# Expert down projection in a hybrid-decoder step: gated values stationary, weights streamed in fp32r halves, two scatters

## The chip, the cores and the metric

The kernel runs on one core of one Trainium2 chip. The metric is the device time of one execution in microseconds, the median over several runs. A difference under 0.3% is not told from none here.

## The reference, cut to what matters

A one-layer decoder step over 1088 tokens (1024 of a prompt, 64 samples): mixers, an output projection, then a mixture of experts, then a norm. The change touches the mixture alone. Each token goes to 2 of 16 experts; an expert is a gated MLP of width 512 on rows of 1024.

```python
def body(acc, params):
    wg, wu, wd, c = params
    y = (jax.nn.silu(x @ wg) * (x @ wu)) @ wd
    return acc + c[:, None] * y.astype(jnp.float32), None

acc, _ = lax.scan(body, jnp.zeros((N, D), jnp.float32), (w_gate, w_up, w_down, combine.T))
```

All inputs and weights are float32. Each expert has 2 MB each of gate, up and down weights.

## The kernel before

**Stages.** `b1_all` and `b2_all` do the mixers, output projection, second norm and router, and write the normed rows to the DRAM tensor `h2_rows` and the residual to `sums`. `b3_all` (L1408) runs the experts, `b4_all` norms the result and writes it out.

**The expert loop.** Every engine runs the same loop, one step for each expert and round. A step handles at most W = 160 of the expert's tokens: 128 as full rows, and W2 = 32 more. It takes 16 steps here (one round of 16 experts). The router has left `rank_m` (each token's place within its expert) and `table` (token numbers and routing weights, in bf16 parts).

- **Indices.** VectorE makes a one-hot matrix `oh` (`onehot`, L1621, a TENSOR_TENSOR compare of `iota_w` with `rank_m`, 2304 elements a partition); TensorE multiplies it with `facts` (`indices`, L1511); VectorE turns the sums into gather indices `idx`, scatter rows `dest` and weights `weight` (`indices`, L1630 to L1646). This runs a step or two ahead, so `dest_now` and `weight_now` (L1686, L1687) keep the copy of the step under way.
- **Gather.** POOL issues three indirect DMAs from `h2_rows` for the next step (L1468): 128 full rows, and twice 128 quarters for the other 32 rows (each row is cut in eight parts of 128, spread over the partitions). Ahead of each gather and scatter it runs a small TENSOR_TENSOR, `hold` (L1481).
- **Rows in.** TensorE transposes the gathered rows (`rows_in`, L1515) and VectorE copies them to `xT` (`x_out`, L1663).
- **Gate and up.** `gate_up(f)` for f = 0 to 3 (L1525): 16 fp32 matmuls of 128 x 128 weights (stationary, from `ring`) with `xT` (160 columns moving). ScalarE takes the Silu into `sg` (L1600), VectorE multiplies into `hid` (L1680). The banks 0 and 1 alternate, so `gate_up(f)` waits until hid(f-2) has been read out. In what follows hid(f) is the VectorE instruction for that f.
- **Down.** `down(j)`, j = 0 to 3 (L1535): eight matmuls each, down weights stationary, `hid` moving (160 columns); the result is transposed (model dimension on the partitions). ScalarE and VectorE copy it to `yT` and `yT2` (L1604, L1695).
- **Rows back.** `rows_back(h)` (L1546) transposes `yT` back to token rows, ScalarE scales with the routing weight into `yr` and `yr2` (L1615).
- **Scatter.** POOL issues three indirect DMAs that add to `sums` (L1475): 512 KB, and two of 64 KB in 512-byte parts. Then it waits until all have landed (`e_out`, L1503) and only then raises `e_free`. VectorE waits for `e_free` at f = 0 before it overwrites `dest_now`, and ScalarE before it overwrites `yr`.
- **Weights.** SP loads the next expert's weights in six transfers of 1 MB (L1453 to L1459): units 0 to 3 into `ring` (0 and 1 after gate_up(1), 2 and 3 after gate_up(3)), 4 and 5 (the two halves of `w_down`, by columns) into `wdn`, 4 after down(1), 5 after down(3). They are issued in the order 0 to 5, each behind its wait.

**Order within a step on TensorE.** gate_up 0 to 3, down 0, down 1, `rows_in` for the next step, down 2, `rows_back(0)`, down 3, `indices`, `rows_back(1)`. On VectorE: `onehot`, hid(0), then the wait for `e_free`, `dest_now`, `indices`, `lower`, then hid(1) to hid(3), yT copies and `x_out`. Each engine works its own list in order, and all waits are on semaphores written out by hand.

On fp32r: a float32 operand cast to that type is rounded; the output projection in `b2_all` (L1194 to L1196) splits each operand into a rounded half (`hi`, by a ScalarE cast) and the remainder (`lo`, by a VectorE subtraction) and adds three products.

Of the kernel before, what the change touches and what calls it, by code (L numbers as in the profile page):

```python
# [22 lines left out]
P = 128  # L23
D = 1024
# [1374 lines left out]
def expert_unit(A, ring, wdn, u, e):  # L1399

    if u < 4:
        w = (A["w_gate"], A["w_up"])[u % 2].rearrange("l e (k p) n -> (l e) p k n", p=P)
        return ring[:, u, :, :], w[e, :, :, (u // 2) * 256:(u // 2 + 1) * 256]
    w = A["w_down"].rearrange("l e (k p) n -> (l e) p k n", p=P)
    return wdn[:, u - 4, :].rearrange("p (k n) -> p k n", k=4), w[e, :, :, (u - 4) * 512:(u - 3) * 512]


def b3_all(nc, A, sb, sem, e_w, ring, wdn, bank, ident, h2_dram, sums_dram, rank_m, table, iota_w, steps):  # L1408
# [13 lines left out]
    dest = sb("dest", [P, 3], I32, ctx=c3)  # L1422
    dest_now = sb("dest_now", [P, 3], I32, ctx=c3)
# [4 lines left out]
    hid = sb("hid", [P, 4, W], ctx=c3)  # L1428
    yT = sb("yT", [P, KC, P], ctx=c3)
    yT2 = sb("yT2", [P, KC, W2], ctx=c3)  # L1430
    yr = sb("yr", [P, D], ctx=c3)
    yr2 = sb("yr2", [P, 2, P], ctx=c3)
# [9 lines left out]
    e_yt, e_ya, e_yd = sem("e_yt"), sem("e_ya"), sem("e_yd")  # L1442
    e_yr, e_re, e_out = sem("e_yr"), sem("e_re"), sem("e_out")
# [18 lines left out]
    def _(pool):  # L1462
        h2_parts = h2_dram.rearrange("t (c d) -> (t c) d", d=P)
        sums_parts = sums_dram.rearrange("t (c d) -> (t c) d", d=P)
# [27 lines left out]
        with pool.Fori(0, n) as i:  # L1492
# [14 lines left out]
    def _(pe):  # L1507
# [7 lines left out]
        def rows_in():  # L1515
            for h in range(2):
                for k in range(4):
                    x = nc.tensor.transpose(bank[4 + h][:, k * P:(k + 1) * P],
# [16 lines left out]
        def down(j, i):  # L1535
            for q in range(2):
                d = 2 * j + q
                for k in range(4):
                    if j == 0 and q == 0 and k >= 2:
                        pe.wait_ge(e_h, i * 4 + k + 2)  # L1540
                    x = nc.tensor.matmul(bank[2 + j % 2][:, q * 256:q * 256 + W],  # L1541
                                         wdn[:, d // 4, k * 512 + (d % 4) * P:k * 512 + (d % 4 + 1) * P],
                                         hid[:, k, :], start=k == 0, stop=k == 3)
            x.then_inc(e_yt, 1)

        def rows_back(h):  # L1546

            for k in range(4):
                x = nc.tensor.transpose(bank[4 + h][:, k * P:(k + 1) * P], yT[:, 4 * h + k, :], ident[:])  # L1549
            x.then_inc(e_yr, 1)  # L1550
            nc.tensor.transpose(bank[6][:, h * P:(h + 1) * P], yT2[:, 4 * h:4 * h + 4, :], ident[:]).then_inc(e_yr, 1)
# [9 lines left out]
        with pe.Fori(0, n) as i:  # L1561
            pe.wait_ge(e_xe, i * 3 + 3)
            for f in range(4):
                pe.wait_ge(e_h, i * 4 + (1 if f < 2 else f))
# [4 lines left out]
            for j in range(4):  # L1569

                pe.wait_ge(e_ya if j % 2 == 0 else e_yd, i * 2 + j // 2 + 1)
                if j % 2 == 0:
                    pe.wait_ge(e_w[4 + j // 2], i * 16 + 16)
                down(j, i)
                if j == 1:
                    pe.wait_ge(e_xg, i * 48 + 96)
                    pe.wait_ge(e_re, i * 4 + 1)
                    rows_in()
                elif j == 2:
                    pe.wait_ge(e_xe, i * 3 + 6)  # L1580
                    pe.wait_ge(e_ya, i * 2 + 2)
                    pe.wait_ge(e_yd, i * 2 + 2)
                    rows_back(0)
# [3 lines left out]
            pe.wait_ge(e_ya, i * 2 + 3)  # L1587
            pe.wait_ge(e_yd, i * 2 + 3)
            pe.wait_ge(e_re, i * 4 + 3)
            rows_back(1)  # L1590

    @blk.scalar
    def _(act):
        n = count(act)
        act.sem_inc(e_ya, 1)
        act.sem_inc(e_re, 1)
        with act.Fori(0, n) as i:
            for f in range(4):
                act.wait_ge(e_gu, i * 4 + f + 1)
                nc.scalar.activation(sg[:, f % 2, :], bank[f % 2][:, 0:W], ACT.Silu).then_inc(e_si, 1)  # L1600
            for j in (0, 2):
                act.wait_ge(e_yt, i * 4 + j + 1)
                y = bank[2][:, :].rearrange("p (q t) -> p q t", q=2)
                nc.scalar.copy(yT[:, 2 * j:2 * j + 2, :], y[:, :, 0:P])  # L1604
                nc.scalar.copy(yT2[:, 2 * j:2 * j + 2, :], y[:, :, P:W]).then_inc(e_ya, 1)
            act.wait_ge(e_free, i + 1)
            act.wait_ge(e_now, i * 2 + 2)
            for h in range(2):
                for c in range(2):
                    act.wait_ge(e_yr, i * 4 + 2 * h + c + 1)  # L1610
                    if c == 0:
                        dst, src = yr[:, h * 512:(h + 1) * 512], bank[4 + h][:, :]
                    else:
                        dst, src = yr2[:, h, :], bank[6][:, h * P:(h + 1) * P]
                    nc.scalar.activation(dst, src, ACT.Copy, scale=weight_now[:, c:c + 1]).then_inc(e_re, 1)  # L1615

    @blk.vector
    def _(dve):
# [11 lines left out]
        def indices(s):  # L1630
# [12 lines left out]
            for where, out in ((to, dest), (tok, idx)):  # L1643
                nc.vector.tensor_copy(out[:, 0:1], where[:, 0:1])
                x = nc.vector.scalar_tensor_tensor(out=out[:, 1:3], in0=where[:, 1:2].broadcast_to([P, 2]),
                                                   scalar=float(KC), in1=chunk[:], op0=ALU.mult, op1=ALU.add)  # L1646
            x.then_inc(e_idx, 1)

        n = count(dve)
        dve.sem_inc(e_h, 1)  # L1650
        dve.sem_inc(e_yd, 1)
# [22 lines left out]
        with dve.Fori(0, n) as i:  # L1674
# [109 lines left out]
```

## Time and profile before

| | |
|---|---|
| runs of the kernel | 1059.4, 1059.9, 1062.76 us; median 1059.9 |
| profiled execution, span from first to last instruction | 1055.8 us |
| TensorE matmul busy | 948.9 us, 90% |
| VectorE busy | 398.3 us, 38% |
| ScalarE busy | 294.9 us, 28% |
| POOL busy | 153.7 us, 15% |
| HBM read, written | 141.18 MB, 25.31 MB |
| mean granted TensorE clock over the span | 0.944 |

The profile is of one execution; its span is 4.1 us under the median of the runs. Busy time is the union of an engine's instructions; matmuls are pipelined, so the distance between the starts of two tells more than their length. The views used here are the page (40 slices), the timeline (instructions in order, with runs of like ones merged), groups by line, waits, and windows (busy time, clock and DMA share of a stretch).

### The profile page before, as it was taken

To read this page: it belongs to the slowest core of one execution; us is meant where nothing else is said; L and a number is where in the kernel's file an instruction comes from. 1 tells how busy PE (TensorE), PEld (TensorE's weight loads), DVE (VectorE), ACT (ScalarE), POOL (GpSimd) and SP (SyncE) were. 2 spreads that over 40 slices of the span, in tenths; PEclk is the share of its full clock that TensorE was granted. 3 is DMA by queue.
4 is the path that set the end of the run, shared out by engine and by line. 5 is a ranking of instruction groups with operands and counts; after the bars stand their busy time and mean duration, and the time that the engine had idled before them with its cause. 6 is when DMAs were issued, how large, how long until landed. Compare 5 with 4: busy or idle time off the path is not lost. (4 is left out here: it accounts for less than half of the span.)

```text
span 1055.8 us, 15299 instructions
## 1 busy us (share of the span) xinstructions
PE 948.9 (90%) x5909; PEld 814.1 (77%) x5909; DVE 398.3 (38%) x977; ACT 294.9 (28%) x573; POOL 153.7 (15%) x173
## 2 busy tenths in 40 slices
PE   5997999999999979999279999999999999999940
PEld 3567776667676658787179999999999999999930
DVE  4236733435664553543632222122222222122204
ACT  4346312443353331543101111112111121112115
POOL 1000000000000010000022322333332322233310
PEclk9998998999999979999579999999999999999975
DMA  8210105101010172543028888888878888887619
GB/s 281 94 41 1 40 1 119 34 7 41 1 40 1 46 240 77 196 163 120 21 85 235 275 266 256 264 240 243 255 237 241 271 267 261 263 245 241 173 23 355
DMA packets 124147, 165.25 MB, mean 157 GB/s; under 512 B 11872, under 2 KB 95872, under 8 KB 124117
## 3 DMA queue, kind: packets, MB, share of 16 engines
q1 hardware_dynamic: 113669, 144.76, 41.4%
q0 software_dynamic: 10448, 20.08, 8.8%
q8 instruction: 20, 0.33, 0.1%
q14 instruction: 10, 0.08, 0.0%
HBM read 141.18 MB, written 25.31 MB: 158 GB/s over the span
## 5 line engine op out<-in xcount | busy, mean ns | idle before, releaser
L1530 PE MATMUL bank<-xT,ring 128*128 128x160 f32 x2048 | 283.9, 301 | 1.8 <-DVE xT L1670 1.0
L1530 PEld LDWEIGHTS bank<-xT,ring 128*128 128x128 f32 x2048 | 280.5, 191 | 5.3 <-issue 5.3
L411 PE MATMUL bank<-hT,ring 128*128 128x384 f32 (+1 forms) x480 | 159.9, 490 | 0.0
L1541 PE MATMUL bank<-hid,wdn 128*128 128x160 f32 x1024 | 150.2, 301 | 0.0
L1541 PEld LDWEIGHTS bank<-hid,wdn 128*128 128x128 f32 x1024 | 141.3, 190 | 2.8 <-DVE hid L1680 2.8
L411 PEld LDWEIGHTS bank<-hT,ring 128*128 128x128 f32 x480 | 94.4, 200 | 57.4 <-issue 11.0
L1600 ACT ACTIVATE sg<-bank 128x160 f32<-128x160 f32 x64 | 19.5, 304 | 252.5 <-PE bank L1530 252.5
L1680 DVE TENSOR_TENSOR hid<-sg,bank 128x160 f32<-128x160 f32 x64 | 20.4, 319 | 163.0 <-ACT sg L1600 163.0
L1475 POOL DMA_INDIRECT sums<-yr,dest_now x48 | 76.2, 1587 | 12.6 <-issue 12.6
L1481 POOL TENSOR_TENSOR hold_at<-ident 128x1 f32<-128x1 f32 x32 | 18.7, 585 | 314.2 <-ACT yr L1615 250.4
L1194 PE MATMUL bank<-whi,ahi 128*128 128x512 f32 (+1 forms) x144 | 58.0, 403 | 6.2 <-DVE wlo L1293 6.1
L1695 DVE COPY yT<-bank 128x256 f32<-128x256 f32 x32 | 13.6, 424 | 124.8 <-PE bank L1541 124.8
L1196 PE MATMUL bank<-whi,alo 128*128 128x512 f32 (+1 forms) x144 | 57.1, 397 | 0.0
L1195 PE MATMUL bank<-wlo,ahi 128*128 128x512 f32 (+1 forms) x144 | 57.1, 397 | 0.0
L1468 POOL DMA_INDIRECT xg<-h_rows,idx x51 | 52.2, 1023 | 24.2 <-issue 20.2
L1621 DVE TENSOR_TENSOR oh<-iota_w,rank_m 128x2304 bf16<-128x2304 f32 x18 | 46.0, 2558 | 0.0
L1604 ACT COPY yT<-bank 128x256 f32<-128x256 f32 x32 | 11.9, 373 | 112.4 <-PE bank L1541 112.4
L1615 ACT ACTIVATE yr<-bank,weight_now 128x512 f32<-128x512 f32 x64 | 30.3, 524 | 41.8 <-PE bank L1549 41.6
L1194 PEld LDWEIGHTS bank<-whi,ahi 128*128 128x128 f32 (+1 forms) x144 | 26.9, 187 | 13.6 <-DVE alo L1287 6.7
L1196 PEld LDWEIGHTS bank<-whi,alo 128*128 128x128 f32 (+1 forms) x144 | 26.7, 186 | 6.9
L1195 PEld LDWEIGHTS bank<-wlo,ahi 128*128 128x128 f32 (+1 forms) x144 | 26.9, 187 | 6.5
L1104 POOL MEMSET before<- 128x128 bf16 x1 | 0.2, 205 | 214.3 <-POOLq L1041 214.3
(284 smaller groups left out, 1201.2 us busy)
## 6 DMA issues: line engine op xcount, KB each, us to landing
wdn<-in_w_down SPq DMA_DIRECT2D x32, 1024.0 KB, 6.9
ring<-in_w_gate SPq DMA_DIRECT2D x32, 1024.0 KB, 5.3
ring<-in_w_up SPq DMA_DIRECT2D x32, 1024.0 KB, 8.0
x<-in_x_prompt SPq DMA_DIRECT2D x16, 512.0 KB, 7.1
ring<-in_w_in SPq DMA_DIRECT2D x8, 1024.0 KB, 8.6
ring<-in_w_out SPq DMA_DIRECT2D x4, 1024.0 KB, 5.0
h_rows<-h SPq DMA_DIRECT2D x8, 512.0 KB, 2.7
sums<-x SPq DMA_DIRECT2D x8, 512.0 KB, 3.6
```

What stands on the lines that cost most here:

```text
L411: mm = nc.tensor.matmul(acc(n)[:, 0:tn], ring[:, u % 4, k, c0:c0 + P], hT[:, k, t0:t0 + tn], start=k == 0, stop=k == KC - 1)
L1194: nc.tensor.matmul(out, ahi[:, s, k, 0:r], whi[:, k, :], start=k == 0, stop=False)
L1195: nc.tensor.matmul(out, ahi[:, s, k, 0:r], wlo[:, k, :], start=False, stop=False)
L1196: m = nc.tensor.matmul(out, alo[:, s, k, 0:r], whi[:, k, :], start=False, stop=k == KC - 1)
L1468: nc.gpsimd.indirect_dma_start(out=dst, out_offset=None, in_=src, in_offset=bass.IndirectOffsetOnAxis(ap=idx[:, j:j + 1], axis=0)).then_in ...
L1475: nc.gpsimd.indirect_dma_start(out=dst, in_=src, in_offset=None, bounds_check=rows - 1, out_offset=bass.IndirectOffsetOnAxis(ap=dest_now[: ...
L1530: x = nc.tensor.matmul(bank[f % 2][:, side * 256:side * 256 + W], ring[:, u, k, c0:c0 + P], xT[:, k, :], start=k == 0, stop=k == KC - 1)
L1541: x = nc.tensor.matmul(bank[2 + j % 2][:, q * 256:q * 256 + W], wdn[:, d // 4, k * 512 + (d % 4) * P:k * 512 + (d % 4 + 1) * P], hid[:, k, ...
L1600: nc.scalar.activation(sg[:, f % 2, :], bank[f % 2][:, 0:W], ACT.Silu).then_inc(e_si, 1)
L1615: nc.scalar.activation(dst, src, ACT.Copy, scale=weight_now[:, c:c + 1]).then_inc(e_re, 1)
L1621: nc.vector.tensor_tensor(oh[:], iota_w[:].unsqueeze(1).broadcast_to([P, TT, 2 * P]), rank_m[:, bass.ds(e * TT, TT)].unsqueeze(2).broadcas ...
L1680: nc.vector.tensor_tensor(hid[:, f, :], sg[:, f % 2, :], bank[f % 2][:, 256:256 + W], ALU.mult).then_inc(e_h, 1)
```

## The change

- The down projection is turned round. `hid` becomes the stationary operand and the down weights stream, 512 columns at a time, so the result has token rows on the partitions, and `rows_back`, `yT` and `yT2` go.
- Both operands are split in fp32r halves. Weights: `wdhi` by a ScalarE copy of 128 x 1024, `wdlo` by a VectorE subtraction, four of each a step; here called cast(f) and wdlo(f). Gated values: `hs` holds hi of 128 tokens, hi of the 32 others, lo of the 32, lo of the 128; a ScalarE copy and two small VectorE subtractions for each f, called hs(f) and lo(f). For each k and each half of the columns there are five matmuls: hi·whi, hi·wlo, lo·whi for 128 tokens, and for the other 32 a stationary operand of 64 columns (their hi and lo beside one another) with whi and wlo.
- Eviction: ScalarE scales rows 32 to 63 of the second bank into `yll` and the 128 rows into `yr`; VectorE scales rows 0 to 31, adds `yll`, and writes `yl`. Two of each a step.
- Two scatters (512 KB and 128 KB) take the place of three; `dest` has two columns, and two index operations go.
- `w_down` is loaded by rows (4 KB runs) instead of by columns (2 KB). SP's order becomes 4, 0, 1, 5, 2, 3; unit 4 waits for wdlo(1), unit 5 for wdlo(3).
- `rows_in` uses the banks 0 and 1 and waits for hid(3).

```diff
-    return wdn[:, u - 4, :].rearrange("p (k n) -> p k n", k=4), w[e, :, :, (u - 4) * 512:(u - 3) * 512]
+    return wdn[:, u - 4, :].rearrange("p (k n) -> p k n", k=2), w[e, :, 2 * (u - 4):2 * (u - 3), :]
...
-            for u in range(6):
-                sp.wait_ge(e_gu if u < 4 else e_yt, i * 4 + (2 if u in (0, 1, 4) else 4))
+            for u in (4, 0, 1, 5, 2, 3):
+                sp.wait_ge(e_gu if u < 4 else e_wl, i * 4 + (2 if u in (0, 1, 4) else 4))
...
+            for j, (src, r) in enumerate(((yr[:], P), (yl[:], W2))):
+                nc.gpsimd.indirect_dma_start(out=sums_dram, in_=src, in_offset=None, bounds_check=N - 1,
+                                             out_offset=bass.IndirectOffsetOnAxis(ap=dest_now[0:r, j:j + 1], axis=0),
...
-            pool.wait_ge(e_re, i * 4 + 5)
+            pool.wait_ge(e_ye, i * 2 + 3)
+            pool.wait_ge(e_yl, i * 2 + 3)
...
-            pool.wait_ge(e_out, i * 48 + 48)
+            pool.wait_ge(e_out, i * 32 + 32)
...
+        def down(k):
+            hi, lo, last = hs[:, k, 0:P], hs[:, k, W + W2:2 * W], hs[:, k, P:W + W2]
+            for h in range(2):
+                whi, wlo = [w[:, k, h * 512:(h + 1) * 512] for w in (wdhi, wdlo)]
+                nc.tensor.matmul(bank[2 + h][:, :], hi, whi, start=k == 0, stop=False)
+                nc.tensor.matmul(bank[2 + h][:, :], hi, wlo, start=False, stop=False)
+                nc.tensor.matmul(bank[2 + h][:, :], lo, whi, start=False, stop=k == 3)
+                nc.tensor.matmul(bank[4 + h][0:2 * W2, :], last, whi, start=k == 0, stop=False)
+                x = nc.tensor.matmul(bank[4 + h][0:2 * W2, :], last, wlo, start=False, stop=k == 3)
+                if k == 3:
+                    x.then_inc(e_y, 1)
...
-                pe.wait_ge(e_h, i * 4 + (1 if f < 2 else f))
+                if f >= 2:
+                    pe.wait_ge(e_h, i * 4 + f - 1)
...
+            for k in range(4):
+                pe.wait_ge(e_wl, i * 4 + k + 1)
+                pe.wait_ge(e_hl, i * 4 + k + 1)
+                if k == 0:
+                    pe.wait_ge(e_ye, i * 2 + 1)
+                    pe.wait_ge(e_yl, i * 2 + 1)
+                down(k)
+                if k == 1:
+                    pe.wait_ge(e_xg, i * 48 + 96)
+                    pe.wait_ge(e_h, i * 4 + 4)
+                    rows_in()
...
             for f in range(4):
+                if f % 2 == 0:
+                    act.wait_ge(e_w[4 + f // 2], i * 16 + 16)
+                nc.scalar.copy(wdhi[:, f, :], wdn[:, f // 2, (f % 2) * D:(f % 2 + 1) * D]).then_inc(e_wh, 1)
                 act.wait_ge(e_gu, i * 4 + f + 1)
                 nc.scalar.activation(sg[:, f % 2, :], bank[f % 2][:, 0:W], ACT.Silu).then_inc(e_si, 1)
+                act.wait_ge(e_h, i * 4 + f + 1)
+                nc.scalar.copy(hs[:, f, 0:W], hid[:, f % 2, :]).then_inc(e_hh, 1)
...
+                act.wait_ge(e_y, i * 2 + h + 1)
+                nc.scalar.activation(yll[:, h * 512:(h + 1) * 512], bank[4 + h][W2:2 * W2, :], ACT.Copy,
+                                     scale=weight_now[W2:2 * W2, 1:2]).then_inc(e_yll, 1)
+                nc.scalar.activation(yr[:, h * 512:(h + 1) * 512], bank[2 + h][:, :], ACT.Copy,
+                                     scale=weight_now[:, 0:1]).then_inc(e_ye, 1)
...
             for f in range(4):
+                dve.wait_ge(e_wh, i * 4 + f + 1)
+                nc.vector.tensor_tensor(wdlo[:, f, :], wdn[:, f // 2, (f % 2) * D:(f % 2 + 1) * D],
+                                        wdhi[:, f, :].bitcast(F32), ALU.subtract).then_inc(e_wl, 1)
                 dve.wait_ge(e_si, i * 4 + f + 1)
-                nc.vector.tensor_tensor(hid[:, f, :], sg[:, f % 2, :], bank[f % 2][:, 256:256 + W],
+                nc.vector.tensor_tensor(hid[:, f % 2, :], sg[:, f % 2, :], bank[f % 2][:, 256:256 + W],
                                         ALU.mult).then_inc(e_h, 1)
+                dve.wait_ge(e_hh, i * 4 + f + 1)
+                nc.vector.tensor_tensor(hs[:, f, W:W + W2], hid[:, f % 2, P:W], hs[:, f, P:W].bitcast(F32), ALU.subtract)
+                nc.vector.tensor_tensor(hs[:, f, W + W2:2 * W], hid[:, f % 2, 0:P], hs[:, f, 0:P].bitcast(F32),
+                                        ALU.subtract).then_inc(e_hl, 1)
...
+            x_out(i * 3 + 3)
+            for h in range(2):
+                dve.wait_ge(e_yll, i * 2 + h + 1)
+                nc.vector.scalar_tensor_tensor(out=yl[:, h * 512:(h + 1) * 512], in0=bank[4 + h][0:W2, :],
+                                               scalar=weight_now[0:W2, 1:2], in1=yll[:, h * 512:(h + 1) * 512],
+                                               op0=ALU.mult, op1=ALU.add).then_inc(e_yl, 1)
```

## Rows read from the trace of the kernel before

**Rows 1.** The page, part 2: 40 equal slices of the span, busy tenths and granted clock.

```profile
PE   5997999999999979999279999999999999999940
...
PEclk9998998999999979999579999999999999999975
```

**Rows 2.** Timeline of TensorE, one step: start us, us, engine, line, operation.

```profile
717.70 17.62 PE L1530 MATMUL bank<-xT,ring 128*128 128x160 f32 x128
735.16 4.71 PE L1541 MATMUL bank<-hid,wdn 128*128 128x160 f32 x32
739.70 1.04 PE L1518 MATMUL bank<-ident,xg 128*128 128x128 f32 x8
...
740.80 2.34 PE L1541 MATMUL bank<-hid,wdn 128*128 128x160 f32 x16
742.97 0.60 PE L1549 MATMUL bank<-ident,yT 128*128 128x128 f32 x4
...
743.52 2.34 PE L1541 MATMUL bank<-hid,wdn 128*128 128x160 f32 x16
745.69 0.60 PE L1511 MATMUL bank<-facts,oh 128*128 128x5 bf16 x18
746.55 0.63 PE L1549 MATMUL bank<-ident,yT 128*128 128x128 f32 x4 [0.26 <-issue]
...
747.33 12.87 PE L1530 MATMUL bank<-xT,ring 128*128 128x160 f32 x93
```

**Rows 3.** Waits, 560 to 1000 us: us in total, times, longest us.

```profile
DVE dest_now L1686 <- POOLq L1503: 58.6, 15, 4.3
```

**Rows 4.** Timeline of all engines from 734 to 766 us.

```profile
746.66 2.56 DVE L1621 TENSOR_TENSOR oh<-iota_w,rank_m 128x2304 bf16<-128x2304 f32 x1
...
748.24 1.03 POOL L1481 TENSOR_TENSOR hold_at<-ident 128x1 f32<-128x1 f32 x1 [15.23 <-ACT yr L1615]
...
749.42 1.62 POOL L1475 DMA_INDIRECT sums<-yr,dest_now  x1 [0.15 <-issue]
...
756.48 0.37 SPq L1459 DMA_DIRECT2D ring<-in_w_gate  x1
...
756.58 0.17 DVE L1686 COPY dest_now<-dest 128x3 int32<-128x3 int32 x1 [3.96 <-POOLq L1503]
...
758.00 0.31 DVE L1680 TENSOR_TENSOR hid<-sg,bank 128x160 f32<-128x160 f32 x1
```

**Rows 5.** Timeline of TensorE in the output projection, fp32r, 512 columns.

```profile
454.04 0.39 PE L1194 MATMUL bank<-whi,ahi 128*128 128x512 f32 x1
...
454.72 0.39 PE L1194 MATMUL bank<-whi,ahi 128*128 128x512 f32 x1
...
459.34 0.49 PE L1194 MATMUL bank<-whi,ahi 128*128 128x512 f32 x1
```

**Rows 6.** Groups by line and shape: busy us, mean ns, idle before.

```profile
L1615 ACT ACTIVATE yr<-bank,weight_now 128x512 f32<-128x512 f32 x32 | 22.0, 688 | 41.8 <-PE bank L1549 41.6
...
L1253 ACT ACTIVATE h<-x 128x1024 f32<-128x1024 f32 x8 | 8.5, 1058 | 33.2 <-DVE x L1303 33.2
...
L1001 DVE TENSOR_TENSOR gT<-gT,v 128x1024 f32<-128x1024 f32 x4 | 4.7, 1218 | 2.5 <-ACT gT L710 2.5
```

**Rows 7.** Timeline at the start of the expert stage, VectorE and POOL.

```profile
526.74 2.55 DVE L1621 TENSOR_TENSOR oh<-iota_w,rank_m 128x2304 bf16<-128x2304 f32 x1
...
527.04 3.28 POOL L1468 DMA_INDIRECT xg<-h_rows,idx  x1 [3.94 <-DVE idx L1645]
...
530.63 0.96 POOL L1468 DMA_INDIRECT xg<-h_rows,idx  x1 [0.30 <-issue]
```

**Rows 8.** Windows: busy us of each engine (count), granted clock, DMA share, GB/s.

```profile
757.70:766.50 8.80, 8.80 (x66) 8.63 (x65) 1.25 (x8) 0.61 (x2) 3.14 (x4) 1.00 0.96 316
...
760.70:761.70 1.00, 1.00 (x10) 1.00 (x9) 0.32 (x1) 0.25 (x1) 0.70 (x2) 1.00 1.10 367
...
1017.50:1021.50 4.00, 0.00 (x0) 0.00 (x0) 0.00 (x0) 0.00 (x0) 3.14 (x2) 0.50 0.88 132
```

More of the change, by code:

```diff
@@ L1421, in b3_all @@
     to = sb("to", [P, 2], ctx=c3)
-    dest = sb("dest", [P, 3], I32, ctx=c3)
-    dest_now = sb("dest_now", [P, 3], I32, ctx=c3)
+    dest = sb("dest", [P, 2], I32, ctx=c3)
+    dest_now = sb("dest_now", [P, 2], I32, ctx=c3)
     weight = sb("weight", [P, 2], ctx=c3)
@@ L1427, in b3_all @@
     hold_at = sb("hold_at", [P, 1], ctx=c3)
-    hid = sb("hid", [P, 4, W], ctx=c3)
-    yT = sb("yT", [P, KC, P], ctx=c3)
-    yT2 = sb("yT2", [P, KC, W2], ctx=c3)
+    hid = sb("hid", [P, 2, W], ctx=c3)
+    hs = sb("hs", [P, 4, 2 * W], F32R, ctx=c3)
+    wdhi = sb("wdhi", [P, 4, D], F32R, ctx=c3)
+    wdlo = sb("wdlo", [P, 4, D], F32R, ctx=c3)
     yr = sb("yr", [P, D], ctx=c3)
-    yr2 = sb("yr2", [P, 2, P], ctx=c3)
+    yl = sb("yl", [W2, D], ctx=c3)
+    yll = sb("yll", [W2, D], ctx=c3)
     e_oh, e_ix, e_idx = sem("e_oh"), sem("e_ix"), sem("e_idx")
@@ L1533, in gate_up @@
             x.then_inc(e_gu, 1)
[L1535 to L1551, printed above, removed]
+        def down(k):
[9 more added lines that the diff above has]
+                    x.then_inc(e_y, 1)
         n = count(pe)
@@ L1568, in _ @@
                 gate_up(f)
[L1569 to L1575, printed above, removed]
+            for k in range(4):
[6 more added lines that the diff above has]
+                if k == 1:
                     pe.wait_ge(e_xg, i * 48 + 96)
-                    pe.wait_ge(e_re, i * 4 + 1)
+                    pe.wait_ge(e_h, i * 4 + 4)
                     rows_in()
[L1579 to L1583, printed above, removed]
             pe.wait_ge(e_oh, i + 3)
@@ L1586, in _ @@
             indices()
[L1587 to L1590, printed above, removed]
     @blk.scalar
@@ L1594, in _ @@
         n = count(act)
-        act.sem_inc(e_ya, 1)
-        act.sem_inc(e_re, 1)
+        act.sem_inc(e_ye, 1)
         with act.Fori(0, n) as i:
             for f in range(4):
+                if f % 2 == 0:
+                    act.wait_ge(e_w[4 + f // 2], i * 16 + 16)
+                nc.scalar.copy(wdhi[:, f, :], wdn[:, f // 2, (f % 2) * D:(f % 2 + 1) * D]).then_inc(e_wh, 1)
                 act.wait_ge(e_gu, i * 4 + f + 1)
                 nc.scalar.activation(sg[:, f % 2, :], bank[f % 2][:, 0:W], ACT.Silu).then_inc(e_si, 1)
[L1601 to L1605, printed above, removed]
+                act.wait_ge(e_h, i * 4 + f + 1)
+                nc.scalar.copy(hs[:, f, 0:W], hid[:, f % 2, :]).then_inc(e_hh, 1)
             act.wait_ge(e_free, i + 1)
@@ L1608, in _ @@
             for h in range(2):
[L1609 to L1615, printed above, removed]
+                act.wait_ge(e_y, i * 2 + h + 1)
[3 more added lines that the diff above has]
+                                     scale=weight_now[:, 0:1]).then_inc(e_ye, 1)
     @blk.vector
@@ L1642, in indices @@
             dve.wait_ge(e_far, s * 3 + 3)
[L1643 to L1647, printed above, removed]
+            nc.vector.tensor_copy(dest[:], to[:])
+            nc.vector.tensor_copy(idx[:, 0:1], tok[:, 0:1])
+            nc.vector.scalar_tensor_tensor(out=idx[:, 1:3], in0=tok[:, 1:2].broadcast_to([P, 2]), scalar=float(KC),
+                                           in1=chunk[:], op0=ALU.mult, op1=ALU.add).then_inc(e_idx, 1)
         n = count(dve)
-        dve.sem_inc(e_h, 1)
-        dve.sem_inc(e_yd, 1)
+        dve.sem_inc(e_yl, 1)
         nc.vector.memset(bank[7][:, 0:2 * PARTS], 0.0)
```

21 lines of the change are left out of this document (5 added, 16 removed).

## The prediction

> **What bounds the kernel now.** The page first, then the TensorE line of the timeline. The page has one long stretch in which TensorE is busy in nearly every slice, at its full clock (2.4 GHz): slices 21 to 38 [rows 1]. That is the expert loop, and the diff touches nothing else. The timeline of one step shows no gap: 17.46 us of gate/up matmuls (717.70 to 735.16), 8.88 us of down matmuls (735.16 to 739.70, 740.80 to 742.97, 743.52 to 745.69), 1.10 us of incoming transposes, 0.55 us for the first half of `rows_back`, 0.86 us for `indices` with the gap behind it, and 0.78 us for the second half with the turn of the loop [rows 2]. Together 29.63 us, 16 times. So TensorE sets the time, and what matters is its stream, and what comes to lie so late that it must wait. I call T the start of a step's first gate/up matmul (717.70, next 747.33) and E the end of its down matmuls (745.69).
>
> One chain runs close beside it, through POOL and VectorE. VectorE waits for `e_free` (last step's scatters landed) before it copies `dest_now`, 15 times, 4.3 us at most [rows 3]. That copy starts at 756.58, T + 9.25 [rows 4]. Behind it on VectorE stands hid(1), and gate_up(3) needs hid(1), at T + 13.1 (three quarters of 17.46). hid(1) ends at 758.31, T + 11.0: 2.1 us of slack.
>
> **TensorE's stream after the change.** Removed: 32 fp32 down matmuls (8.88 us) and ten transposes (0.55 + 0.55; the turn of the loop, 0.23, stays). Added: 40 fp32r matmuls of 512 columns. The output projection has this form: 454.04 to 454.72 is three of them, 0.227 us each [rows 5], so 9.07 us. After another kind of work the first lasts 0.49 instead of 0.39 (459.34) [rows 5]: 0.1, twice a step, 0.2. New step: 17.46 + 9.27 + 1.10 + 0.86 + 0.23 = 28.92 us, 0.71 less, 16 x 0.71 = **11.4 us saved** if nothing waits. Three products instead of full fp32 buy nothing by themselves, since an fp32 matmul of 160 columns takes 8.88/32 = 0.28; the saving is the transposes.
>
> **Work added to the side engines, per step.** ScalarE: four casts of 128x1024 (bound by the 1.06 us of an ACTIVATE of that size [rows 6]) and four small casts (0.3 by my estimate, half an eviction), less four yT copies; its evictions stay four, of 0.69 or less [rows 6]. In a step of 29 us that is hidden; what counts is its place in the chain below. VectorE: four subtractions of 128x1024, 1.22 each [rows 6]; eight small ones, about 0.4 a pair; two evictions of 512 columns (0.69, as for the eviction on ScalarE); less two pairs of yT copies and two index operations (0.07 each, hidden or not). All would fit if order did not matter. It does, at two places.
>
> **Place one: the port and the chain of e_free.** At start-up the one-hot compare, a TENSOR_TENSOR with both inputs in SBUF, runs 526.74 to 529.29; a gather issued at 527.04 takes 3.28 us instead of 0.96, so it ends 1.03 after the compare [rows 7]. In the loop the compare runs 746.66 to 749.22 and POOL's `hold` starts at 748.24 and ends at 749.27 [rows 4]: POOL stands until VectorE is through. The Trainium skill (SBUF — State Buffer, Who interferes with whom) says that a DVE instruction with two SBUF inputs contends with a GpSimd instruction that reads SBUF, and that the second one to issue fully blocks. By that rule both stalls are the lock, the rows agree, and the new subtractions of that kind will hold POOL too; the same page infers that descriptor generation needs only the write interface, which would spare the scatter, and by that the time would be rival A's, 1048.
> Walk it from E. The last down matmul ends at about E + 0.16 (0.39 long at a pitch of 0.23 [rows 5]). ScalarE, busy with yr(0), starts yll(1) at E + 0.25 and ends it at E + 0.94; VectorE's yl(1) ends at E + 1.7. Only now does the compare start: E + 1.75 to E + 4.3, where before it ended at 749.22, E + 3.53. Behind it on VectorE is now wdlo(0), which has its cast long ago: E + 4.3 to E + 5.5. Even where `hold` slips between them, the scatter comes 0.15 us after `hold` [rows 4] and meets wdlo(0). So the first scatter is free at E + 5.55 and issued by E + 7.15 (1.62 long), before 751.04, E + 5.35. From there to `e_free` it was 756.58 - 751.04 = 5.54 us with three scatters. In the last step, where no weights are moved, the engines are busy from 1017.5 to 1021.5 for them [rows 8], so most of it is the 512 KB of the first; the two 64 KB ones give way to one of 128 KB. I leave it at 5.5. `dest_now` at E + 12.65. T is now E + 0.86 + 0.23 = E + 1.09, so it stands at **T + 11.6** instead of T + 9.25.
> Then: indices and `lower` 1.42 less 0.07 (756.58 to 758.00 [rows 4]), wdlo(1) 1.22, hid(1) 0.32: hid(1) ends at T + 14.5, and gate_up(3), due at T + 13.1, waits **1.4 us**. The first step has no scatter before it: 15 x 1.4 = 21 us. Bounds: 0 if VectorE's subtractions do not hold the scatter (hid(1) then ends about T + 12.9), and 0.4 if POOL's waiting instruction is let in first each time; above, 2.2, if the small subtractions and the second scatter block each other in turn. I take 1.4, since the nearest rows [rows 4, 7] show POOL blocked whole.
>
> **Place two: the gathers behind the weights.** The diff also reorders SP. Loads 0 and 1 waited for gate_up(1) alone (issued at 756.48 [rows 4]); now they stand behind load 4, which waits for wdlo(1), at `dest_now` + 2.6. So three loads of 1 MB go out just ahead of the three gathers. Before, two loads (2.1 MB) and the gathers (0.66 MB) moved 2.8 MB between 757.7 (1.2 after the issue) and 766.5 at 316 GB/s, and in the full part at some 360 [rows 8]. The rows do not say who goes first. `rows_in` wants the gathers at `dest_now` + 2.9 + 4.36 + 4.54 = + 11.8. With transfers starting 1.2 after the issue, as there, at + 3.9: one load and the gathers are through by + 3.9 + 4.7 = + 8.6, two loads by + 11.5, all three (3.8 MB) by + 14.5. Wait between 0 and 2.7 us a step, 3 with the landing. I take 0.1, the middle order, and keep 3 for the range. The loads themselves are in time: u1 lands at T + 26 and is wanted at T + 30; 5, 2 and 3 follow within 9 us, by next T + 5, and are wanted at next T + 8.7.
> The other moved waits cost nothing: down(0) has its halves since T + 8 (no wait for the last hid, which cost 0.17 before), `rows_in` needs hid(3), done by T + 22 against T + 23.5.
>
> **Tail and sum.** One scatter fewer, and no compare in the last step: 0.7 us saved. -11.4 - 0.7 + 21 + 1.5 = +10.4 us. The sum is made against the profiled span of 1055.8 us; the median of the runs is 1059.9, so 4.1 lie around it and I leave them: **1070 us**. A difference under 0.3%, about 3.2 us, counts as none.
>
> **Rivals.**
> A, on the other side: POOL isn't held up by the subtractions, or is let in before them. `dest_now` comes at T + 10 or earlier, gate_up(3) does not wait, and the packed stream remains: 1059.9 - 12 = **1048**. The point at which it decides: `dest_now` before T + 10.2. For it: the slack of 2.1 us, one scatter fewer. Against: [rows 7] and the `hold` of every step. Chance 0.30.
> B: the gathers land behind all three loads, 3 us more in 15 steps: 1070 + 45 = **1115**. For it: SP issues just before POOL. Against: the engines serve both queues, and 2.8 MB before never made `rows_in` wait. Chance 0.12.
> C: half of the stall (0.6 to 0.9 us): the wait eats the saving, 15 x 0.75 against 12, **1059**. Chance 0.13.
> That fp32r runs otherwise than in [rows 5] I hold for excluded, since form and type are the same; the 64-column one is the only new shape.
> My forecast, the stall of a good microsecond: 0.45.
>
> **Range and chances.** A at 1048 with 3 us for the transitions sets the low end, 1045; the forecast's own range is 1062 to 1080; up to half of B is taken in: 1098. Faster is A and little of C: 0.32; same 0.13; slower 0.55.
>
> **What the profile after will show.** Right: 40 matmuls of 512 columns a step at a pitch of 0.227 and a step of 28.9 plus its waits; TensorE idle before gate_up(3) on DVE hid, about 1.4 us, 15 times; `hold` or the first scatter stretched until wdlo(0) ends; `dest_now` near T + 11.6. Wrong: `dest_now` near T + 10 and no idle TensorE (A); idle before the transposes of `rows_in` on the DMA (B); down matmuls that wait for casts or subtractions, which I excluded.

## The result and the profile after

The changed kernel takes 1064.38 us (median of 11 runs, 1062.19 to 1068.67), the kernel before 1059.55 (11 runs, 1057.56 to 1062.76). The ratio is 1.0041, 95% interval 1.0026 to 1.0056: slower, by 4.8 us (2.8 to 5.9 by the interval), where I had forecast 10.4. The stall came where it was expected and nearly as long; but a part of the sum that I had copied as TensorE's work was a wait, and it went too.

The page of the profiled execution (1064.68 us, span 1062.9), parts 1 and 2, answers to [rows 1]:

```profile
PE 945.2 (89%) x5365; PEld 766.6 (72%) x5365; DVE 501.4 (47%) x1120; ACT 395.0 (37%) x653; POOL 174.2 (16%) x157
...
PE   5999999999999979999279999999999999999930
...
PEclk9989999998899979999579999999999999999975
```

TensorE is still busy in every slice of the expert loop and at its full clock, VectorE has gone from 398 to 501 us and ScalarE from 295 to 395. Shares do not tell what happened; the step does. TensorE's timeline of one step (start us, us, engine, line, operation), to be laid beside [rows 2]:

```profile
721.49 13.28 PE L1532 MATMUL bank<-xT,ring 128*128 128x160 f32 x96
735.91 4.61 PE L1532 MATMUL bank<-xT,ring 128*128 128x160 f32 x32 [1.15 <-DVE hid L1668]
740.26 0.50 PE L1542 MATMUL bank<-wdhi,hs 128*128 128x512 f32 x1
...
744.96 1.04 PE L1520 MATMUL bank<-ident,xg 128*128 128x128 f32 x8
...
745.97 0.48 PE L1542 MATMUL bank<-wdhi,hs 128*128 128x512 f32 x1
...
750.65 0.61 PE L1513 MATMUL bank<-facts,oh 128*128 128x5 bf16 x18
751.34 0.92 PE L1532 MATMUL bank<-xT,ring 128*128 128x160 f32 x5
```

With T = 721.49 and E = 720.79 (the `indices` before it), the step is 29.85 us. Gate/up takes 18.77 us up to the first down matmul. Without a stall it is 17.36 in this kernel (17.35 and 17.36 in e7 and e9 below; 17.46 in the kernel before), so the stall before gate_up(3) is 1.41 here, and 1.32 in the mean of 15 steps. The down matmuls take 4.70 + 4.68 = 9.38, `rows_in` 1.01, and from the end of the down matmuls to the next gate/up it is 0.69. Over the 14 steps behind the first the mean is 29.77, before it was 29.64. The stall's row in the waits of 560 to 1010 us (us in total, times, longest), with the one that answers to [rows 3]:

```profile
DVE dest_now L1678 <- POOLq L1505: 78.2, 15, 5.8
...
PEld bank L1532 <- DVE hid L1668: 19.4, 15, 1.8
```

And the chain behind it, the timeline of all engines, which answers to [rows 4]:

```profile
720.79 0.61 PE L1513 MATMUL bank<-facts,oh 128*128 128x5 bf16 x18
...
722.74 2.56 DVE L1608 TENSOR_TENSOR oh<-iota_w,rank_m 128x2304 bf16<-128x2304 f32 x1
722.87 2.48 POOL L1482 TENSOR_TENSOR hold_at<-ident 128x1 f32<-128x1 f32 x1 [13.36 <-DVE yl L1687]
...
725.21 1.22 DVE L1665 TENSOR_TENSOR wdlo<-wdn,wdhi 128x1024 fp32r<-128x1024 f32 x1
725.50 2.44 POOL L1476 DMA_INDIRECT sums<-yr,dest_now  x1 [0.15 <-issue]
...
728.24 1.36 POOL L1476 DMA_INDIRECT sums<-yl,dest_now  x1 [0.30 <-issue]
...
733.06 0.17 DVE L1678 COPY dest_now<-dest 128x2 int32<-128x2 int32 x1 [5.29 <-POOLq L1505]
...
734.41 1.22 DVE L1665 TENSOR_TENSOR wdlo<-wdn,wdhi 128x1024 fp32r<-128x1024 f32 x1
```

Read from the top: the compare starts at E + 1.95, `hold` stands behind it for 2.48 us, wdlo(0) starts as the compare ends, the first scatter starts 0.29 us into wdlo(0) and is 2.44 us long, the second follows, and `dest_now` comes at 733.06, **T + 11.57**. Then come the indices, wdlo(1) at 734.41, hid(1), and only then gate_up(3) at 735.91.

**Where the time is.** From the first gate/up matmul to the last `indices` the kernel before takes 474.65 us (537.79 to 1012.44), the changed one 475.94 (542.33 to 1018.27): 1.3 more. From there to the end of the span it is 43.36 and 44.63: 1.3 more. These are single executions; in e10 below, whose steps are those of the kernel before, the same stretch of the loop takes 475.38, so the first figure is good to most of a microsecond.

The loop starts 4.5 us later in the profiled execution, in stages whose code is the same. That goes with the granted clock. Over the whole span it is 0.944 for the kernel before and 0.938 for the changed one, which is 118 and 132 us at the lower level (1.2 GHz), and the difference lies ahead of the loop: 74.6 against 89.1 us there. Over the 13 profiled executions here and below the loop starts between 537.8 and 544.2, mostly the later the longer the clock was low ahead of it (77.7 us and 537.90 in e9, 90.5 us and 544.16 in e2). The profiled execution of the kernel before was also a fast one: its span of 1055.8 stands for some 1057.6 us (in the other executions 1.7 to 1.9 us lie around the span, not the 4.1 that I had taken), which is the fastest of its eleven runs, 2 us under their median. So 2.6 us are placed. The other 2.2 between the medians are of the size by which the loop's start moves from one execution to the next; no trace shows how they are divided, nor why the clock falls more often in one execution than in another.

### The profile page after: what moved, and what is told of

It reads as the page before. It is cut to its first block and busy times, and to the rows that moved or that the text cites. A ratio compares the mean times of both kernels' runs of the same rounds, so it can differ in the third digit from the quotient of the medians.

```text
span 1062.9 us, 14384 instructions
## 1 busy us (share of the span) xinstructions
PE 945.2 (89%) x5365; PEld 766.6 (72%) x5365; DVE 501.4 (47%) x1120; ACT 395.0 (37%) x653; POOL 174.2 (16%) x157
## 5 line engine op out<-in xcount | busy, mean ns | idle before, releaser
L1532 PEld LDWEIGHTS bank<-xT,ring 128*128 128x128 f32 x2048 | 280.5, 191 | 23.1 <-DVE hid L1668 19.4
L1482 POOL TENSOR_TENSOR hold_at<-ident 128x1 f32<-128x1 f32 x32 | 54.7, 1711 | 304.7 <-DVE yl L1687 217.2
L1665 DVE TENSOR_TENSOR wdlo<-wdn,wdhi 128x1024 fp32r<-128x1024 f32 x64 | 78.2, 1222 | 17.7 <-ACT wdhi L1590 17.7
L1599 ACT ACTIVATE yll<-bank,weight_now 32x512 f32<-32x512 f32 x32 | 21.8, 681 | 126.9 <-PE bank L1546 126.5
L1590 ACT CAST wdhi<-wdn 128x1024 fp32r<-128x1024 f32 x64 | 66.7, 1042 | 0.2
L1542 PE MATMUL bank<-wdhi,hs 128*128 128x512 f32 x128 | 53.4, 417 | 0.0
L1687 DVE SCALAR_TENSOR_TENSOR yl<-bank,weight_now,yll 32x512 f32<-32x512 f32 x32 | 23.6, 739 | 62.0 <-ACT yll L1599 62.0
L1652 DVE COPY xT<-bank 128x512 f32<-128x512 f32 x34 | 22.0, 687 | 60.3 <-PE bank L1520 60.3
L1543 PE MATMUL bank<-wdlo,hs 128*128 128x512 f32 x128 | 50.4, 394 | 0.0
L1544 PE MATMUL bank<-wdhi,hs 128*128 128x512 f32 x128 | 50.0, 390 | 0.0
L1546 PE MATMUL bank<-wdlo,hs 128*64 128x512 f32 x128 | 49.9, 390 | 0.0
L1545 PE MATMUL bank<-wdhi,hs 128*64 128x512 f32 x128 | 49.9, 390 | 0.0
L1592 ACT ACTIVATE sg<-bank 128x160 f32<-128x160 f32 x64 | 19.4, 303 | 67.2 <-PE bank L1532 67.0
```

The source lines that it names most:

```text
L1482: nc.gpsimd.tensor_tensor(hold_at[:], ident[:, 0:1], ident[:, 1:2], ALU.add).then_inc(e_hold, 1)
L1532: x = nc.tensor.matmul(bank[f % 2][:, side * 256:side * 256 + W], ring[:, u, k, c0:c0 + P], xT[:, k, :], start=k == 0, stop=k == KC - 1)
L1542: nc.tensor.matmul(bank[2 + h][:, :], hi, whi, start=k == 0, stop=False)
L1543: nc.tensor.matmul(bank[2 + h][:, :], hi, wlo, start=False, stop=False)
L1544: nc.tensor.matmul(bank[2 + h][:, :], lo, whi, start=False, stop=k == 3)
L1590: nc.scalar.copy(wdhi[:, f, :], wdn[:, f // 2, (f % 2) * D:(f % 2 + 1) * D]).then_inc(e_wh, 1)
```

## The experiments

T, E, cast, wdlo and hid as in the prediction. "Step" is the mean over the 14 steps behind the first of the profiled execution. The ratio is to the kernel before, run beside them, with its interval.

| kernel | median us | ratio | step us |
|---|---|---|---|
| before | 1060.6 / 1060.4 / 1060.1 (three sessions) | | 29.64 |
| changed | 1064.38 | 1.0041 (1.0026 to 1.0056) | 29.77 |
| e1 hid(1) first | 1057.29 | 0.9968 (0.9954 to 0.9982) | 29.59 |
| e2 wdlo(0) late | 1050.72 | 0.9912 (0.9895 to 0.9928) | 29.06 |
| e3 hid first | 1047.91 | 0.9878 (0.9862 to 0.9895) | 28.96 |
| e4 wdlo small | 1049.37 | 0.9904 (0.9871 to 0.9936) | 29.01 |
| e5 hid first, loads back | 1052.81 | 0.9941 (0.9913 to 0.9968) | 29.16 |
| e6 loads back | 1065.05 | 1.0047 (1.0027 to 1.0067) | 30.01 |
| e7 one-hot late | 1042.38 | 0.9841 (0.9802 to 0.9879) | 28.48 |
| e8 before, indices twice | 1059.99 (one run) | | 29.64 |
| e9 loads after gathers | 1041.03 | 0.9821 (0.9799 to 0.9842) | 28.46 |
| e10 before, one-hot late | 1059.58 | 0.9995 (0.9980 to 1.0011) | 29.64 |
| e11 wdlo(0) twice | 1063.51 | 1.0025 (1.0010 to 1.0040) | 29.84 |

**e1, hid(1) before wdlo(1).**

```diff
             for f in range(4):
-                wdlo(f); hid(f)
+                (hid(f); wdlo(f)) if f == 1 else (wdlo(f); hid(f))
```

(Here and below the VectorE code of the diff is abbreviated to its names.)

> VectorE does hid(1) before wdlo(1); all else as in the changed kernel. Theory (chain of e_free, then wdlo(1), then hid(1)): dest_now stays at T + 11.6, hid(1) ends 1.22 us earlier, at T + 13.2, the wait before gate_up(3) falls from 1.33 to about 0.1 us in 15 steps, the time falls by 18 us to about 1046. Rival (TensorE waits for something else that comes at the same time, the scatter or a transfer of weights): no change, 1064.

1057.3, not 1046. The waits of the weight loads in 560 to 1010 us:

```profile
PEld bank L1520 <- issue: 15.2, 14, 1.5
...
PEld bank L1532 <- DVE hid L1669: 4.1, 9, 0.8
```

and that of the matmuls themselves before `rows_in`:

```profile
PE bank L1520 <- DMA xg<-h_rows,idx: 8.6, 14, 1.0
```

The stall before gate_up(3) shrank as the theory says, from 19.4 us to 4.1 in total. But nearly as much turned up before `rows_in` (L1520, its weight loads idle 15.2 us in 14 steps, the matmuls' row names the gathers). `dest_now` is still at T + 11.73 (731.02 against 719.29), so the gathers are as late as they were, and there is nothing left to cover them. This is the second limit that I had priced at 0.1.

**e2, hid(0) before wdlo(0).** The same edit with `f == 0`.

> VectorE does hid(0) before wdlo(0); wdlo(1) still ahead of hid(1). Theory (POOL's scatter is held by wdlo(0), since it stands directly behind the compare): the first scatter instruction shrinks from 2.44 to 1.6 us, dest_now comes 0.84 us earlier, at T + 10.7, the wait before gate_up(3) falls to 0.5 us, 12 to 13 us less, 1052. Rival (only the load of VectorE counts, and the scatter is long because it is long): scatter still 2.4 us, dest_now still at T + 11.6, 1064.

The group of the first scatter, by shape (busy us, mean ns of one, idle time before):

```profile
L1476 POOL DMA_INDIRECT sums<-yr,dest_now x16 | 26.1, 1633 | 2.9 <-issue 2.9
```

and the timeline of a step, in which `dest_now` and the start of gate_up(3) are to be seen:

```profile
720.52 13.28 PE L1532 MATMUL bank<-xT,ring 128*128 128x160 f32 x96
...
731.52 0.17 DVE L1683 COPY dest_now<-dest 128x2 int32<-128x2 int32 x1 [4.07 <-POOLq L1505]
...
734.37 4.61 PE L1532 MATMUL bank<-xT,ring 128*128 128x160 f32 x32 [0.57 <-DVE hid L1669]
```

The first scatter is 1.63 us as expected, `dest_now` comes at T + 11.0 in this step and at T + 10.8 in the mean of 15 (expected 10.7; 11.5 in the changed kernel), and the time is 1050.7 (expected 1052). Nothing was taken from VectorE here, only moved by one place. The rival, that only VectorE's load counts, falls.

**e3, both.** hid(f) before wdlo(f) for every f.

> hid(f) before wdlo(f) for all f, the two edits together. Theory: no wait before gate_up(3) at all, a packed step of 28.5 us, 15 x 1.33 = 20 us less than the changed kernel: 1044, and 15 under the kernel before. Rival (a second limit lies just behind, the gathers behind three loads or the casts): the wait turns up before rows_in or a down matmul, and the time stays above 1055.

1047.9: the stall before gate_up(3) is gone, and `rows_in` waits. The waits of its matmuls in 560 to 1010 us:

```profile
PE bank L1520 <- DMA xg<-h_rows,idx: 4.3, 9, 0.6
```

and the timeline of one step:

```profile
724.95 0.17 DVE L1678 COPY dest_now<-dest 128x2 int32<-128x2 int32 x1 [3.99 <-POOLq L1505]
...
736.61 1.09 PE L1520 MATMUL bank<-ident,xg 128*128 128x128 f32 x8 [0.36 <-DMA xg<-h_rows,idx]
```

Both sides had a part: the theory on the first stall, the rival on the second. `rows_in` starts 11.7 us after `dest_now` here (736.61), as soon as the gathers have landed. In the changed kernel it starts at + 11.9 (744.96 against 733.06), behind the stall, and in the steps behind the first its own gathers land at + 10.9 to + 11.6 (mean 11.2), so it never waits for them.

**e4, no lower halves.**

```diff
-                nc.vector.tensor_tensor(wdlo[:, f, :], wdn[...], wdhi[:, f, :].bitcast(F32), ALU.subtract)
+                nc.vector.tensor_tensor(wdlo[:, f, 0:8], wdn[...], wdhi[:, f, 0:8].bitcast(F32), ALU.subtract)
...
-                whi, wlo = [w[:, k, h * 512:(h + 1) * 512] for w in (wdhi, wdlo)]
+                whi, wlo = [w[:, k, h * 512:(h + 1) * 512] for w in (wdhi, wdhi)]
```

> Leaves out the lower halves of the weights: wdlo is computed for 8 of 1024 columns and the upper halves are streamed twice, so TensorE and all transfers do the same work. Theory: VectorE is 1.05 us shorter at both places, first scatter 1.6 us, dest_now near T + 10.7, hid(1) at T + 12.6, no wait, 1044, the same as with hid first. Rival (the port isn't the matter): dest_now at T + 11.6 and a wait of about 0.3 us, 1049.

1049.4, with `dest_now` at T + 10.8 (727.13 against 716.33) and a first scatter of 1.63 us. It is e3's picture by another way: no wait on hid, and idle weight loads before `rows_in`:

```profile
PEld bank L1520 <- issue: 11.0, 13, 1.5
```

Taking the four large subtractions away gains no more than moving them (e3). So they cost nothing as work; they cost by where they stand.

**e5, e3 with the loads in their old order.**

```diff
-            for u in (4, 0, 1, 5, 2, 3):
+            for u in (0, 1, 4, 2, 3, 5):
```

> As e3 (hid before wdlo everywhere), and SP's order is 0, 1, 4, 2, 3, 5, so the loads of ring 0 and 1 leave right behind gate_up(1) and only two loads stand before the gathers. Theory (what is left in e3 is the landing of the gathers behind three loads): the wait before rows_in, 0.3 to 0.5 us a step in e3, goes, the step is packed at 28.5 us, 5 to 8 us under e3, about 1041. Rival (the gathers are late by their own issue, POOL held by VectorE): the wait before rows_in stays and the time is that of e3, 1048.

Worse, not better: 1052.8. The theory as I had put it (three loads ahead of the gathers are one too many) falls. Timeline:

```profile
724.75 0.37 SPq L1462 DMA_DIRECT2D ring<-in_w_gate  x1
...
729.24 0.37 SPq L1462 DMA_DIRECT2D wdn<-in_w_down  x1
...
732.22 0.95 POOL L1470 DMA_INDIRECT xg<-h_rows,idx  x1 [0.31 <-issue]
...
733.40 0.37 SPq L1462 DMA_DIRECT2D ring<-in_w_gate  x1
...
738.68 1.09 PE L1520 MATMUL bank<-ident,xg 128*128 128x128 f32 x8 [0.84 <-DMA xg<-h_rows,idx]
```

The loads 0 and 1 leave earlier now, but so do 4 and 2: load 4 at 729.24 lies between the first gather and the others, and load 2 at 733.40 follows the last gather at once. `rows_in` starts 5.5 us after the last gather was issued (733.17 to 738.68), and the gathers had landed 0.1 before; over the steps they land 4.4 to 5.7 us after that issue (mean 5.0), 4.9 in the changed kernel.

**e6, the loads' old order in the changed kernel.** The same edit alone.

> The changed kernel with SP's order 0, 1, 4, 2, 3, 5 alone. Theory: in the changed kernel the wait before gate_up(3) covers the late gathers (rows_in starts only 0.2 us after they land), so the order of the loads costs nothing there: no change beyond 2 us, 1064. Rival (the loads share the transfer engines with the scatter and delay e_free): dest_now moves by half a microsecond or more, and the time by 8 us or more, one way or the other.

1065.05 against 1064.38, no change between the medians. `rows_in` waits a little in 2 steps of 15, so the stall before gate_up(3) does cover the late gathers, and SP's new order is not what made the changed kernel slower. But `dest_now` comes at T + 11.67 in the mean (11.98 at most), 0.2 later than the 11.48 of the changed kernel, and the profiled step is 30.01 us against 29.77. That is 3.4 us over 14 steps in one execution each, so a small gain by the new order is neither shown nor excluded.

**e7, the compare behind the four hid.**

```diff
-            onehot((i + 2) % NE)
             for f in range(4):
...
-                    dve.wait_ge(e_oh, i + 3)
-                    lower((i + 2) % NE)
+            onehot((i + 2) % NE)
+            dve.wait_ge(e_oh, i + 3)
+            lower((i + 2) % NE)
             x_out(i * 3 + 3)
```

> The changed kernel with the one-hot compare moved from the head of the step to behind the four hid, where VectorE waits anyway; wdlo stays before hid. Theory (hold and scatter stand behind compare and wdlo(0)): hold is no longer 2.48 us long, the first scatter is issued about 2.5 us earlier, dest_now at T + 9.1, hid(1) at T + 11.9, no wait before gate_up(3) nor before rows_in, a packed step of 28.5 us, 1044. Rival (only wdlo(1) ahead of hid(1) matters, or the compare is needed early by TensorE): dest_now moves and the time doesn't, or TensorE waits at indices for the compare.

1042.4, and TensorE packed at 28.44 to 28.50 us in every step behind the first. Timeline:

```profile
741.28 17.63 PE L1532 MATMUL bank<-xT,ring 128*128 128x160 f32 x128
...
742.61 0.19 POOL L1482 TENSOR_TENSOR hold_at<-ident 128x1 f32<-128x1 f32 x1 [14.70 <-DVE yl L1687]
743.35 1.63 POOL L1476 DMA_INDIRECT sums<-yr,dest_now  x1 [0.55 <-issue]
...
744.79 1.23 DVE L1664 TENSOR_TENSOR wdlo<-wdn,wdhi 128x1024 fp32r<-128x1024 f32 x1 [2.33 <-ACT wdhi L1590]
...
750.09 0.17 DVE L1677 COPY dest_now<-dest 128x2 int32<-128x2 int32 x1 [2.58 <-POOLq L1505]
...
758.63 0.50 PE L1542 MATMUL bank<-wdhi,hs 128*128 128x512 f32 x1
```

`hold` is 0.19 us long, and the scatter starts 2.81 us after E (740.54) rather than 4.71. `dest_now` stands at T + 8.8. With wdlo(1) ahead of hid(1) as ever, TensorE does not wait, at `rows_in` neither, since the gathers too are issued earlier: what decided was when the scatter could go. VectorE now waits 2.33 us for the cast of wdlo(0), which ScalarE starts only after its evictions; the subtraction starts at 744.79, when the issue of the first scatter (743.35, 1.63 long) is nearly over.

**e8, the kernel before with the small matmuls of `indices` done twice.**

```diff
-            indices()
+            for r in range(2):
+                (the 18 matmuls of indices)
+            x.then_inc(e_ix, 1)
```

> The kernel before, with the 18 small matmuls of indices done twice in each step (0.6 us more of them). It asks what the 0.26 us of idle time behind indices is that I counted as part of indices. If it is a wait for the last yT copy of VectorE, the second set fills it and the step grows by 0.6 - 0.26 = 0.34 us, 29.97; if it is the cost of issuing after small matmuls, the gap stays and the step grows by 0.6 to 30.23.

Neither: the step stays at 29.64 us (29.63 to 29.70 in the 14 steps of the one execution that was taken). The timeline, to be laid beside [rows 2]:

```profile
718.09 1.05 PE L1589 MATMUL bank<-facts,oh 128*128 128x5 bf16 x36
...
718.63 0.21 DVE L1701 COPY yT<-bank 128x64 f32<-128x64 f32 x1
...
719.00 0.64 PE L1549 MATMUL bank<-ident,yT 128*128 128x128 f32 x4
...
719.73 17.62 PE L1530 MATMUL bank<-xT,ring 128*128 128x160 f32 x128
```

and VectorE's last yT copy in the kernel before:

```profile
746.24 0.21 DVE L1696 COPY yT<-bank 128x64 f32<-128x64 f32 x1
```

Two sets now fit into 0.91 us, where one stood in 0.86 (745.69 to 746.55), and the transposes start 0.05 later, which the turn of the loop takes up. So a set takes about 0.45 us (its 18 matmuls added 1.05 - 0.60 to the row), and 0.41 of my 0.86 were a wait. The semaphore that the transposes wait for is raised by VectorE's last yT copy, which ends 0.10 us before them in the kernel before (746.45) and 0.16 here (718.84). The wait is only partly visible as a gap: the row of the small matmuls is 0.60 long, 0.15 more than a set takes of the stream.

**e9, e5 with SP waiting for the gathers.**

```diff
             for u in (0, 1, 4, 2, 3, 5):
+                if u == 4:
+                    sp.wait_ge(e_xg, i * 48 + 96)
```

> As e5, and SP waits until the three gathers have landed before it issues load 4 (and 2, 3, 5 behind it). e3 and e5 wait 0.5 to 0.8 us before rows_in for gathers that land 5 to 5.5 us after their last issue. Theory (they land late because loads 4, 2 and 3 stand in the transfer engines when they arrive): the landing comes within 3 us of the last issue, the wait before rows_in goes, packed steps of 28.5, about 1042; the delayed loads have time until the next step. Rival (the landing is slow by itself or by loads 0 and 1): the wait before rows_in stays, and the time is 1048 to 1053 or more.

1041.0, packed at 28.46. Timeline:

```profile
727.82 0.95 POOL L1472 DMA_INDIRECT xg<-h_rows,idx  x1 [0.30 <-issue]
...
731.83 0.37 SPq L1464 DMA_DIRECT2D wdn<-in_w_down  x1
...
732.82 1.04 PE L1522 MATMUL bank<-ident,xg 128*128 128x128 f32 x8
```

The last gather is issued by 728.77, and SP's next load, which waits for the landing, leaves at 731.83: 3.1 us. Over the 14 steps behind the first it is 1.7 to 3.1, mean 2.5, where e5 took 5.0. One wait added on SP is worth 12 us against e5. The loads that stand near the gathers delay them, and the loads themselves are in time. The wait holds back loads 4, 2, 3 and 5 together, so it does not say which of them counts.

**e10, the compare late in the kernel before.** The edit of e7 on it.

> The kernel before with the one-hot compare moved to behind the four hid, the move that gave e7 its time. Theory (the kernel before never waits for this chain, TensorE is packed at 29.64 us a step): dest_now comes earlier and nothing else changes, within 2 us of 1060. Rival (the move is a gain by itself and would have helped before too): 1050 or less.

1059.58 and a step of 29.64: no change, with `dest_now` at T + 8.7 in the mean. The gain of e7 belongs to the changed kernel.

**e11, wdlo(0) twice.**

```diff
+                if f == 0:
+                    nc.vector.tensor_tensor(spare[:], wdn[...], wdhi[:, f, :].bitcast(F32), ALU.subtract)
                 wdlo(f)
```

> The changed kernel with the subtraction of wdlo(0) done once more, into a spare tile, directly ahead of it. Theory (POOL's first scatter stands until VectorE is through with the whole run of such subtractions): the first scatter instruction is 3.6 us instead of 2.44, dest_now 1.2 us later, the wait before gate_up(3) 2.5 instead of 1.3 us, 17 us more, 1082. Rival (POOL is let in between two subtractions): scatter 2.4 us long or less, dest_now unchanged within 0.3 us, 1065 to 1068.

The rival is right: the time is 1063.5. Timeline:

```profile
721.03 1.22 DVE L1667 TENSOR_TENSOR spare<-wdn,wdhi 128x1024 fp32r<-128x1024 f32 x1
721.32 2.44 POOL L1477 DMA_INDIRECT sums<-yr,dest_now  x1 [0.15 <-issue]
...
722.17 1.22 DVE L1669 TENSOR_TENSOR wdlo<-wdn,wdhi 128x1024 fp32r<-128x1024 f32 x1
...
728.84 0.17 DVE L1682 COPY dest_now<-dest 128x2 int32<-128x2 int32 x1 [4.45 <-POOLq L1506]
```

The scatter is 2.44 us long, as with one subtraction, although the second (722.17) follows the first without a gap. `dest_now` is at T + 11.49 (717.35), and at T + 11.5 in the mean as in the changed kernel. POOL waits for the one instruction that it ran into, and not for the next.

## Why the prediction was wrong, point by point

**The step that failed: the stream, mis-sized by 7 us.** The mechanism was right and one term of the sum was not. I took "1.10 + 0.86 + 0.23" over from the old step as work that stays. The 0.86 from the start of `indices` to the second half of `rows_back` held 0.41 us of waiting for the yT copy (e8), and that copy goes with the change. The new end of a step is 0.45 + 0.23 = 0.68, measured 0.69. The other parts of the stream moved by a tenth each: gate/up 17.36 for 17.46, `rows_in` 1.01 for 1.10, the down matmuls 9.38 for 9.27. The packed stream is therefore 28.5 us (e7 and e9), not 28.92, and the saving 1.2 us a step, not 0.71: some 7 us more over the loop. I had seen the 0.26 us marked "issue" and named it a gap, without asking what it waited for.

**The chain of e_free: right in place and size.** The first scatter was issued by E + 7.15 to the hundredth (727.94), `dest_now` came at T + 11.57 where I had 11.6, and the stall was 1.3 us a step where I had 1.4 (19.4 us of idle weight loads where I had 21). e2, e4 and e7 each took one thing out of that chain and moved the end with it. Small errors cancelled: the compare started at E + 1.95, not E + 1.75, from the scatter's issue to `e_free` it was 5.12 us, not 5.54, and T lies 0.69 behind E, not 1.09.

**Why POOL stood: right, with two corrections.** `hold` stood behind the compare and the first scatter behind wdlo(0), so rival A, in which the scatter is spared, did not come true. `hold` did slip between the two, as I had it. But POOL is held by the one instruction that it runs into and not through a run of them (e11), so a longer queue behind would have cost nothing more. And wdlo(0) did not have "its cast long ago": ScalarE ended that cast at 725.02 (its row is 723.97, 1.05 us), only 0.28 us before the compare ended at 725.30.

**The gathers: the risk was real, the price was covered.** I charged 0.1 us a step; the changed kernel shows none, for rows_in comes at `dest_now` + 11.9 and they land at + 10.9 to + 11.6. That is luck: the margin is 0.3 to 1.0 us, and without the stall of 1.3 there would be none. As soon as the stall is mended without moving `dest_now` by more than 0.8 us (e1, e3, e4, e5), they bound the step; in e7, where `dest_now` comes 2.7 us earlier, they do not. My picture of three loads ahead of them was wrong: load 4 leaves with the first gather (735.84 and 735.83) and loads 0 and 1 behind it, and with all three in flight the gathers land by + 11.6, not + 14.5. Putting loads 0 and 1 ahead made it worse (e5). That the loads near the gathers delay them is shown by e9; which of them, and why e5 is slower than e3, stays open.

**The tail.** I had 0.7 us saved and it was 1.3 more. The first scatter's issue ends 10.75 us before SP's first load of the last stage in the kernel before (1017.35 to 1028.10), and 12.41 in the changed one (1022.71 to 1035.12), with the transfers over by 1023 and by 1027: nothing moves in between. The stretch behind the last `indices` is 0.7 to 1.6 us longer in each of the ten profiled kernels with the new down projection than in the three with the old one, so it is no chance of one execution; what the stage's start waits for there stays open, as do some 2 us before the loop.

**The sum again**, for the loop up to the last `indices`: -15 x 1.18 for the whole steps and -0.25 for the last, which ends there (27.75 for 28.00), +19.8 for the stall (15 x 1.32) and -0.5 for the first gate/up, which ran partly at 1.2 GHz in both (1.47 us over its packed time, 1.93 before): +1.4 us; measured 475.94 - 474.65 = 1.3. I had -11.4 + 21 + 1.5 = +11.1 for it, and -0.7 for the tail, where it was +1.3. Rival A's price, 1048, was too high by the same 6 to 7 us: the same kernel without the stalls takes 1041 to 1042.

## What to carry to other kernels

Before you carry a stretch of the old stream over into the new sum, ask of every stretch between two of its operations whether it is work or a wait that the change removes; doubling the cheap work in it tells the two apart. When VectorE gets more work, look first at where it stands relative to what POOL issues and to what a chain needs next: here moving one compare was worth 22 us and letting hid(0) pass wdlo(0) 14, and taking the work away gave no more than moving it. And transfers that a step waits for should not be issued into the middle of those that it doesn't; a wait on SP can be a gain.

## What the runs showed of the hardware

- A POOL instruction that reads SBUF, issued during a VectorE TENSOR_TENSOR with two SBUF inputs, stood until that instruction ended (`hold` 2.48 us behind the compare instead of 0.19; first scatter 2.44 instead of 1.63 behind wdlo(0)), but the next such instruction, queued without a gap, did not hold it (e11), nor was VectorE delayed: the second subtraction was again 1.22 us long.
- The Trainium skill (SBUF — State Buffer, Who interferes with whom) says that a VectorE instruction with two SBUF inputs contends with a POOL instruction that reads SBUF, and that the order of issue decides who blocks; the trace agrees. Its inference that descriptor generation needs the write interface, and so escapes a TENSOR_TENSOR, does not carry over to the issue of this scatter: taken whole, it was 0.81 us longer. Which part of it was held is not shown.
- A gather's landing depends on the bulk loads around it: the last of three landed 1.7 to 3.1 us after its issue (mean 2.5) with no new load near it (e9), 4.4 to 5.7 us (mean 5.0) with loads 4 and 2 around it (e5).
- With the same code in front, the expert loop started anywhere from 537.8 to 544.2 us in 13 executions, and TensorE had been at 1.2 GHz for 74.6 to 90.5 us before it.
